# A hybrid encoder layer on one core: paired attention heads, and a feed-forward that takes its RMS root after the first product

## The reference

```python
xn = rms_norm(x, norm_mix_g)
q, k, v, gu, gv, z, xbc, dt_raw, gates = split(xn @ w_in)
y_a = window_attention(q, k, v, ...)     # 8 heads of 64, 2 key groups, blocks of 128, window of 3 blocks
y_b = spatial_gating(gu, gv, ...)        # chunks of 128
y_c = ssd_branch(z, xbc, dt_raw, ...)    # forward and backward scans over chunks of 128
merged = sig(g0) * (y_a @ w_up_attn) + sig(g1) * (y_b @ w_up_gmlp) + sig(g2) * (y_c @ w_up_ssd)
h = x + merged @ w_out
hn = h * rsqrt(mean(h * h) + eps) * norm_ff_g
return h + square(relu(hn @ w_ff1)) @ w_ff2
```

## Time and profile before

| | |
|---|---|
| median of 3 runs | 2713.98 us (2712.83 to 2716.47) |
| profiled execution, and its span | 2711.97 us, 2710.0 us |
| busy, share of the span | PE 2507.7 us (93%), DVE 1263.9 (47%), ACT 652.3 (24%), POOL 680.4 (25%) |
| mean granted TensorE clock | 0.967 |
| chain of waits, shares | PE lines L156 to L158 10% each, DVE L1868 1%, L298 1% |

### The profile page before, as it was taken

How to read it: one execution, slowest core, us unless ns; L and a number is a source line. 1 busy time by engine, 2 the same in 40 slices (tenths; PEclk the granted TensorE clock), 3 DMA queues, 4 the chain that set the end, 5 groups by cost and what they waited for, 6 DMA issues and landing times. The chain is left out here.

```text
span 2710.0 us, 33078 instructions
## 1 busy us (share of the span) xinstructions
PE 2507.7 (93%) x12924; PEld 2037.7 (75%) x12924; DVE 1263.9 (47%) x1723; ACT 652.3 (24%) x1055; POOL 680.4 (25%) x294
## 2 busy tenths in 40 slices
PE   3999999899998999799939898969999999999999
PEld 1877887666666888688718787848888888888887
DVE  5310355244443877577642385364334243342433
ACT  5321232244543222122251212141101011010110
POOL 3232333211110000000024332343333333333332
PEclk8999999999999999899969999979999999999999
DMA  3112332322222344466424333101111111111112
GB/s 111 49 64 71 127 119 79 108 86 86 85 79 95 132 166 163 158 204 195 150 93 156 109 136 128 39 16 40 39 39 39 36 34 39 39 39 39 39 35 89
DMA packets 142866, 240.29 MB, mean 89 GB/s; under 512 B 9707, under 2 KB 100779, under 8 KB 140108
## 3 DMA queue, kind: packets, MB, share of 16 engines
q1 hardware_dynamic: 142796, 239.34, 26.3%
HBM read 176.99 MB, written 62.32 MB: 88 GB/s over the span
## 5 line engine op out<-in xcount | busy, mean ns | idle before, releaser
L187 POOL TENSOR_TENSOR w_hi<-w_raw,masks_sb 128x1024 fp32r<-128x1024 f32 x126 | 304.2, 2414 | 1352.4 <-PE acc L158 737.6
L156 PE MATMUL acc<-r_hi,w_hi 128*128 128x512 f32 (+1 forms) x960 | 344.5, 359 | 34.5 <-DVE r_lo L322 24.1
L157 PE MATMUL acc<-r_hi,w_lo 128*128 128x512 f32 (+1 forms) x960 | 343.1, 357 | 0.0
L158 PE MATMUL acc<-r_lo,w_hi 128*128 128x512 f32 (+1 forms) x960 | 342.5, 357 | 0.0
L190 POOL TENSOR_TENSOR w_lo<-w_raw,w_hi 128x1024 fp32r<-128x1024 f32 x126 | 324.8, 2578 | 9.9
L156 PE MATMUL acc<-u_hi,w_hi 128*128 128x512 f32 (+1 forms) x768 | 273.9, 357 | 6.7 <-DVE u_lo L1861 6.7
L157 PE MATMUL acc<-u_hi,w_lo 128*128 128x512 f32 (+1 forms) x768 | 272.4, 355 | 0.0
L158 PE MATMUL acc<-u_lo,w_hi 128*128 128x512 f32 (+1 forms) x768 | 271.6, 354 | 0.0
L1875 DVE TENSOR_TENSOR h_T<-h_T,acc 128x512 f32<-128x512 f32 (+1 forms) x192 | 114.4, 599 | 290.4 <-PE acc L158 290.4
L156 PE MATMUL acc<-xn_hi,w_hi 128*128 128x512 f32 (+1 forms) x624 | 224.7, 360 | 9.3 <-DVE xn_lo L322 8.8
L156 PEld LDWEIGHTS acc<-r_hi,w_hi 128*128 128x128 f32 x960 | 183.4, 191 | 65.2 <-issue 32.9
(11 more groups left out here) (249 smaller groups left out, 4741.2 us busy)
## 6 DMA issues: line engine op xcount, KB each, us to landing
w_raw<-in_w_tiles SPq DMA_DIRECT2D x146, 512.0 KB, 3.6
h_T<-s_late_T SPq DMA_DIRECT2D x24, 640.0 KB, 5.3
f_w<-s_ac SPq DMA_DIRECT2D x10, 1024.0 KB, 4.8
b_w<-s_ac SPq DMA_DIRECT2D x10, 1024.0 KB, 4.9
s_xbc_T<-x_T_sb SPq DMA_DIRECT2D x12, 640.0 KB, 3.2
s_late_T<-la_result SPq DMA_DIRECT2D x12, 640.0 KB, 3.6
f_xbc<-s_xbc_T SPq DMA_DIRECT2D x10, 768.0 KB, 4.8
b_xbc<-s_xbc_T SPq DMA_DIRECT2D x10, 768.0 KB, 4.9
```

The costliest lines, as they stand in the source:

```text
L156: pe.matmul(out, w_hi, x_hi, start=first, stop=False)
L157: pe.matmul(out, w_lo, x_hi, start=False, stop=False)
L158: return pe.matmul(out, w_hi, x_lo, start=False, stop=last)
L187: pool.tensor_tensor(self.hi[:, s], self.raw[:, s], self.masks[:, ONES].unsqueeze(1).to_broadcast([P, KD, P]), ALU.mult).then_inc(self.hi_ ...
```

## The change

Attention heads go in pairs (g = 0 and 1 of one j). Both score matmuls of a pair are issued back to back, into the two banks, after one wait for both banks; then come two late k. In `values` two heads are transposed, two late k follow, and the products of the pair alternate head by head for each block b, into partitions 0 to 63 and 64 to 127 of one bank. `PT` has four buffers. DVE and ACT take the heads in the new order.

In `out_product` the weight halves are made by ACT and DVE, and TensorE no longer sums over partitions at its end. In `feed_forward` ACT rounds h x gain directly (r_hi), DVE forms the rest in one instruction (r_lo), and the first product runs on that, not yet normalised. TensorE sums the squares after its first unit, ACT makes the three roots, and DVE applies the root with the relu: `max(acc, 0) * root`, read from PSUM. ACT then squares twice, once rounded (u_hi) and once in full, and DVE subtracts (u_lo). ACT and DVE also make the weight halves, and POOL has no work here. The first block is written out for all engines, the last one for ACT and DVE too. `Normalise` loses its `summed` form, and for the scan branch uses part of `merged` as its room.

```diff
@@ attention_and_gmlp, tensor
-                    for h in range(HEADS):
-                        g, j = h // 4, h % 4
-                        rows_of = slice(g * HD, (g + 1) * HD)
-                        if not (first(chunk) and h < 2):
-                            pe.wait_ge(s_read, chunk * 8 + (h - 1))
-                        pe.matmul(ps_s[:, h % 2, 0:W], q[rows_of, s, j, :], k[rows_of, s, :],
-                                  start=True, stop=True).then_inc(s_full, 1)
-                        between(h)
+                    for j in range(HEADS // 2):
+                        if not (first(chunk) and j == 0):
+                            pe.wait_ge(s_read, chunk * 8 + 2 * j)
+                        for g in range(2):
+                            rows_of = slice(g * HD, (g + 1) * HD)
+                            pe.matmul(ps_s[:, g, 0:W], q[rows_of, s, j, :], k[rows_of, s, :],
+                                      start=True, stop=True).then_inc(s_full, 1)
+                        between(2 * j)
+                        between(2 * j + 1)
...
+                        pe.wait_ge(t_read, chunk * 8 + (2 * j + 2))
                         for b in range(3):
-                            mm = pe.matmul(ps_o[g * HD:(g + 1) * HD, j * P:(j + 1) * P],
-                                           v[:, s, b, g * HD:(g + 1) * HD], PT[:, h % 2, b], start=b == 0, stop=b == 2)
+                            for g in range(2):
+                                mm = pe.matmul(ps_o[g * HD:(g + 1) * HD, j * P:(j + 1) * P],
+                                               v[:, s, b, g * HD:(g + 1) * HD], PT[:, (2 * j + g) % 4, b],
+                                               start=b == 0, stop=b == 2)
...
@@ out_product, scalar (vector has ws.low_half at the start of each f)
+                    if g == 0:
+                        if f:
+                            act.wait_ge(full, 3 * f)
+                        ws.high_half(act, (f + 1) % 2, B_OUT + f + 1)
...
@@ feed_forward, tensor
                             for k in range(KD):
+                                if very_first and i == 0:
+                                    pe.wait_ge(hn_lo, KD * g + k + 1)
                                 mm = three_products(pe, acc1[:, g, 0:n], ws.hi[:, s, k], ws.lo[:, s, k],
                                                     r_hi[:, k, t0:t0 + n], r_lo[:, k, t0:t0 + n], k == 0, k == KD - 1)
                             mm.then_inc(full1, 1)
+                            if very_first and u == 0:
+                                sums_of_squares()
...
@@ feed_forward, scalar
+                for g, (t0, n) in enumerate(GROUPS):
+                    for k in range(KD):
+                        act.activation(r_hi[:, k, t0:t0 + n], h[:, k, t0:t0 + n], ACT.Identity, scale=gain[:, k:k + 1]).then_inc(hn_hi, 1)
+                        if g == 0 and k == KD - 1:
+                            ws.high_half(act, 1, B_FF + 1)
+                act.wait_ge(summed, 1)
...
+                        act.wait_ge(relued, b * U1 + (u + 4))
+                        act.activation(u_hi[:, i, t0:t0 + n], relu[:, u % 2, 0:n], ACT.Square).then_inc(high, 1)
...
+                        act.activation(square[:, u % 2, 0:n], relu[:, u % 2, 0:n], ACT.Square).then_inc(squared, 1)
...
@@ feed_forward, vector
+                        dve.scalar_tensor_tensor(r_lo[:, k, t0:t0 + n], h[:, k, t0:t0 + n], gain[:, k:k + 1],
+                                                 r_hi[:, k, t0:t0 + n].bitcast(F32), ALU.mult, ALU.subtract).then_inc(hn_lo, 1)
+                    if g == 0:
+                        ws.low_half(dve, 1, B_FF + 1)
+                dve.wait_ge(rooted, 3)
...
+                        dve.scalar_tensor_tensor(relu[:, u % 2, 0:n], acc1[:, g, 0:n], 0.0, root[:, t0:t0 + n],
+                                                 ALU.max, ALU.mult).then_inc(relued, 1)
+                        dve.wait_ge(squared, b * U1 + (u + 1))
                         dve.tensor_tensor(u_lo[:, i, t0:t0 + n], square[:, u % 2, 0:n], u_hi[:, i, t0:t0 + n].bitcast(F32),
                                           ALU.subtract).then_inc(low, 1)
```

More of the change, by code:

```diff
@@ L968, in values, with turn @@
                 def values(s, chunk, loads, between):
[L969 to L972, removed]
+                    def turn(i):
+                        pe.wait_ge(p_ready, chunk * 8 + (i + 1))
+                        if not (first(chunk) and i < 2):
+                            pe.wait_ge(t_read, chunk * 8 + (i - 1))
@@ L989, in values @@
                         pe.wait_ge(o_read, chunk)
[L990 to L994, removed]
+                    for j in range(HEADS // 2):
+                        if j + 1 < HEADS // 2:
+                            turn(2 * j + 2)
+                            turn(2 * j + 3)
+                        between(2 * j)
+                        between(2 * j + 1)
+                        mm = products(j)
                     mm.then_inc(o_full, 1)
@@ new lines, in _ @@
+                for g, (t0, n) in enumerate(GROUPS):
+                    for k in range(KD):
[3 more added lines that the diff above has]
+                act.wait_ge(summed, 1)
+                for g, (t0, n) in enumerate(GROUPS):
+                    act.activation(root[:, t0:t0 + n], acc2[:, g, 0:n], ACT.Ln, scale=1.0 / D, bias=consts["eps"][:, 0:1]).then_inc(logged, 1)
@@ L1838, in high_half, with block_of @@
+                act.wait_ge(logged, 3)
+                for g, (t0, n) in enumerate(GROUPS):
+                    act.activation(root[:, t0:t0 + n], root[:, t0:t0 + n], ACT.Exp, scale=-0.5).then_inc(rooted, 1)
+                def block_of(b, very_first=False, last=False):
+                    for u in range(U1):
                         i, g = u // 3, u % 3
                         t0, n = GROUPS[g]
-                        act.wait_ge(squared, b * U1 + (u + 1))
-                        act.activation(u_hi[:, i, t0:t0 + n], square[:, u % 2, 0:n], ACT.Identity).then_inc(high, 1)
@@ L1843, in _ @@
[L1843 to L1851 removed]
+                        if g == 0 and i:
+                            next_half(b, i - 1)
@@ new lines, in block_of @@
+                        act.wait_ge(relued, b * U1 + (u + 4))
+                        act.activation(u_hi[:, i, t0:t0 + n], relu[:, u % 2, 0:n], ACT.Square).then_inc(high, 1)
+                        if not (very_first and u < 2):
+                            act.wait_ge(low, b * U1 + (u - 1))
+                        act.activation(square[:, u % 2, 0:n], relu[:, u % 2, 0:n], ACT.Square).then_inc(squared, 1)
+                    for i in range(KB - 1, TILES - 2 if last else TILES):
+                        next_half(b, i)
```

178 lines of the change are left out of this document (85 added, 93 removed).

## The result

The changed kernel takes 2629.04 us (median of 4 runs, 2626.33 to 2632.93), the kernel before 2713.45 beside it: a ratio of 0.9688, 95% interval 0.9671 to 0.9705. Forecast were 2633 us, in a range of 2612 to 2674. The profiled execution is the longest of the four, 2632.93 us with a span of 2631.1 us.

A forecast was written before the change was run, and what follows sets the result against it. TensorE, busy for 93% of the span, was taken as the bound. From 2711.97 us, attention's 44.4, the output product's 2.2 and the feed-forward's 32.2 were subtracted, giving 2633 us, in a range of 2612 to 2674 (chance 0.82).

The forecast's parts named there:

- Scores: Attention's score matmuls in pairs: 1.6 us saved in each of 9 steps, 14.4 us.
- That is three slots, 1.17 us: A score pair's four records: b1 runs beside a2, so the pair takes three slots, 1.17 us.
- full overlap: Rival for attention's pairs: both heads run wholly at once, score pair 0.84 us, total 2619 us; chance 0.14.
- Values: Attention's value products in pairs, 0.91 us each: 3.0 us saved in each of 10 chunks, 30 us.
- I cost it at nothing: Chunk 0 of attention, with no late work among its scores: no cost.
- Output product: First r_lo no longer slowed by POOL's weight half: 2.2 us of TensorE's 5.47 us wait saved; moved halves cost nothing.
- Feed-forward start: Of 35.9 us lost there, 9.7 remain (3.6 + 2 + 2.2 + 1.9): 26.2 us saved.
- Blocks: Where the second feed-forward matrix begins: 0.85 us of idle time goes in seven blocks, 6.0 us saved.
- Serial pairs: Rival: the halves of the array don't overlap in attention's pairs, total 2663 us; chance 0.13.
- loads in series: Rival: each record of a product pair first waits for its weights, some 0.05 us; total 2680 us; chance 0.07.
- a switch at each alternation: Rival: attention's pairs pay 0.18 or 0.14 us per alternation between halves, total 2698 us; chance 0.05.
- the slower one: Rival: TensorE empties at each alternation in attention's pairs, 0.32 us each, 75.5 us; total 2739 us; chance 0.06.

The follow-up runs named there:

- late_ahead: The changed kernel with five late k instead of two behind a step's first score pair, then 2, 1 and 0: 2605.58 us, 0.9606 of the kernel before.

## Why the prediction was right, and where its steps were not

**Total.** Right to 4 us, in part by luck: attention gained 2.3 us less and the feed-forward 5.1 us more than forecast, and within attention two errors of some 10 us each cancel.

**Scores.** Forecast -14.4, measured 130.1 to 115.7 us over nine steps, -14.4; but by the two errors that cancel. The step that failed is "That is three slots, 1.17 us": a pair takes 0.85, the full overlap of the rival, and pairs stand 2.43 us apart where the clock is full. The fourth score record, forecast about 1 us after the first, starts 0.43 us after it. One step of the nine ran wholly so, with its 4.7 us to the second pair, in 11.9 us, just what the rival gave. What the rival's 2619 lacked, and the forecast too, is the half clock behind the wait, 1.5 us in 7 steps; late_ahead, where the wait is filled, has none in any step. The Trainium skill ("TensorEngine Tiling (Array Packing)", Key Properties) says that tiles operate independently, and this trace agrees: 0.85 us here beside 0.84 for a single head.

**Values.** Forecast -30, measured 135.3 to 103.8, -31.5. Product pairs take 0.81 and not 0.91, and pair periods 2.32 and not 2.43. The start of the values came as forecast: heads 3 and 4 end 607.51 - 604.88 = 2.63 us after the first transpose (2.59), with 1.15 us of waiting.

**First chunk.** "I cost it at nothing" failed. From its first score to the second chunk's first are 37.8 us instead of 33.4, 4.4 us more, and with them attention falls short. Some 1.8 us of it come up to TensorE's first matmul behind the wait in the rows below: a pair needs both banks and no late work lies between, so there are three waits of 1.1 us among the scores, and 3.4 us of half clock behind them. The other 2.6 us come behind that wait, for ScalarE's read-out of the late tile, where the clock is at half for 6.8 us (509.57 to 516.40 us). The kernel before waits at the same place (first row) longer than after (second row), and keeps the full clock:

```profile
507.75 0.47 PE L156 MATMUL la_acc<-xn_hi,w_hi 128*128 128x512 f32 x1 [3.72 <-ACT la_result L767]
```

```profile
510.86 0.77 PE L156 MATMUL la_acc<-xn_hi,w_hi 128*128 128x512 f32 x1 [3.17 <-ACT la_result L763]
```

So the length of a wait alone doesn't decide whether the clock falls. What else decides it, no run here shows.

**Output product.** Forecast -2.2, measured -2.9. TensorE's wait at its start, forecast at 3.3 us, is 4.84 (the second row below): the r_lo of 3.66 us was the second of the eight, not the first, so the first wait fell by 0.63 us only, and the rest of the gain came at the second k, whose wait of 1.87 us is gone. The weight halves cost nothing, as said. TensorE's matmul at the second k, before, and its first matmul of the output product, after:

```profile
1661.87 0.80 PE L156 MATMUL acc<-r_hi,w_hi 128*128 128x512 f32 x1 [1.87 <-DVE r_lo L1545]
```

```profile
1619.05 0.77 PE L156 MATMUL acc<-r_hi,w_hi 128*128 128x512 f32 x1 [4.84 <-DVE r_lo L1551]
```

**Feed-forward start.** Left over were to be 9.7 us; measured are 3.74 us from the table's cut (1734.34) to the first matmul, 3.58 of them idle, and the first block's 115.64 - 110.32 = 5.32, so 9.1. But half clock (1.7 us), sums (1.96) and wait (1.16) are not separate terms, as the sum took them. In late_ahead the first unit ran at full clock, and the wait was 2.77 instead of 1.16; the fourth unit starts 19.0 us after the first matmul in both. ScalarE's chain sets that point, and the other terms only divide the time ahead of it. That the sum came out near is luck in part.

**Blocks.** Forecast seven times 0.85, measured seven times 1.41: the two waits of 0.43 and 0.42 also cost (1.41 - 0.85) / 2 = 0.28 us each beside their idle time, a restart, which the sum left out. These 3.9 us are most of the feed-forward's surplus. The reason given, "POOL has no work now", isn't needed: GpSimd's split alone brings nothing back, and the edits tried bring back 0.3 us of a block at most.

**Rivals.** Serial pairs, loads in series, a switch at each alternation and the slower one fall with the pairs' 0.85 and 0.81 us. Full overlap had the mechanism, and a time 10 us too low.

## What to carry to other kernels

Two half-array matmuls cost as much as one here when they use different rows or columns, so pair them; then ask what must be ready for a pair that a single one didn't need, and put independent work into that wait. Price a wait on TensorE with its restart and with the clock that may fall behind it, not with its idle time alone. Where several terms stand ahead of one late chain on another engine, cost the chain, and nothing ahead of it.

## What the runs showed of the hardware

- Two fp32 matmuls on different halves of the array ran wholly at once, both with split rows and with split columns (0.85 against 0.84 us, 0.81 against 0.80); on the same half they took 1.49 and 1.46.
- Behind a wait of 2.21 us on TensorE the granted clock fell to 1.2 GHz for 3.4 us in 7 of 8 steps of after (5 to 7 in the five kernels with the same attention), behind 1.95 us in 4 of 8, behind 0.89 us in none. A longer wait did not always bring it: in the first chunk the clock fell at a wait of 3.17 us (after) and stayed at 2.4 GHz at one of 3.72 us (before). Where the wait of the steps was filled, it stayed at 2.4 GHz, with transfers running at 301 GB/s.
- In products of two heads on different column halves, issued head after head, the second head's first record started before the first head's third product: 1.07 us for the pair, against 0.81 in turn and 1.46 on the same half.
- Beside GpSimd's split a VectorE subtraction of 128x256 from two SBUF operands took 1.60 us instead of 0.43, while an addition of 128x512 from PSUM kept its 0.69.
